# Stick-breaking attention regrouped by pairs of heads and halves of the queries in a one-core decoder layer

## The reference, cut to what matters

```python
def _stick_breaking(q, k, v):
    scale = 1.0 / math.sqrt(Dh)
    ...
        z = jnp.einsum('bqhd,bkhd->bhqk', qb, k).astype(jnp.float32) * scale
        causal = (s_pos[None, :] < t[:, None])[None, None]
        log_beta = jax.nn.log_sigmoid(z)
        log_keep = jnp.where(causal, jax.nn.log_sigmoid(-z), 0.0)
        after = lax.cumsum(log_keep, axis=3, reverse=True) - log_keep
        a = jnp.where(causal, jnp.exp(log_beta + after), 0.0)
        return jnp.einsum('bhqk,bkhd->bqhd', a.astype(v.dtype), v)
```

## Time and profile before

| | us |
|---|---|
| median of 3 runs (2522.57 to 2524.77) | 2524.6 |
| the profiled execution | 2522.39 |
| its span, first to last instruction | 2520.6 |
| PE, DVE, ACT, POOL busy in the span | 2450.4, 1169.5, 573.5, 194.7 |
| mean granted clock of TensorE | 0.985 |
| first stick-breaking scores to the end of the memory attention's turn 0 | 823.5 to 1154.4 |

### The profile page before, as it was taken

How to read it: one execution, slowest core, us unless ns; L and a number is a source line. 1 busy time by engine, 2 the same in 40 slices (tenths; PEclk the granted TensorE clock), 3 DMA queues, 4 the chain that set the end, 5 groups by cost and what they waited for, 6 DMA issues and landing times.

```text
span 2520.6 us, 25978 instructions
## 1 busy us (share of the span) xinstructions
PE 2450.4 (97%) x10608; PEld 1917.2 (76%) x10608; DVE 1169.5 (46%) x1193; ACT 573.5 (23%) x716; POOL 194.7 (8%) x153
## 2 busy tenths in 40 slices
PE   6999999999999999889999999999999999999998
PEld 5888888888887555446666888878788888888887
DVE  7344444444446556556643533353444444444444
ACT  5211111111104444442413311131311111111111
POOL 2000000000002445330000000001000000000000
PEclk8999999999999999999999999999999999999999
DMA  5211111111113000001102111122111111111112
GB/s 161 73 50 48 44 50 50 50 49 36 48 50 117 17 17 17 9 17 34 34 26 26 55 53 52 50 69 92 49 42 51 50 50 44 48 50 50 50 50 67
DMA packets 48802, 125.80 MB, mean 50 GB/s; under 512 B 4253, under 2 KB 22461, under 8 KB 48480
## 3 DMA queue, kind: packets, MB, share of 16 engines
q1 hardware_dynamic: 45660, 112.88, 14.8%
q10 hardware_dynamic: 2596, 10.89, 1.2%
q0 software_dynamic: 480, 1.10, 0.2%
HBM read 116.42 MB, written 9.87 MB: 50 GB/s over the span
## 4 chain that ended last, share of the span: by engine, by line
PE 91%; DVE 5%; ACT 2%; issue 1%; SPq 1%; DMA 0%; DVEq 0%; ACTq 0%
PE ps L1215 90%; DVE h_lo L808 1%; SPq L453 1%; DVE w_lo L801 0%; PE ps L1516 0%; ACT pr_x L583 0%; ACT pr_x L585 0%; DVE pr_x L915 0%; DVE xT L856 0%; PE ps L1463 0%; DVE d_qk L923 0%; DVE d_qk L918 0%; DVE h_lo L1146 0%; DVE xT L973 0%; DMA raw<-in_weights 0%
## 5 line engine op out<-in xcount | busy, mean ns | idle before, releaser
L1215 PE MATMUL ps<-h_hi,w_hi 128*128 128x512 f32 x2240 | 891.5, 398 | 11.5 <-DVE h_lo L808 3.8
L1215 PE MATMUL ps<-h_lo,w_hi 128*128 128x512 f32 x2240 | 876.2, 391 | 0.0
L1215 PE MATMUL ps<-h_hi,w_lo 128*128 128x512 f32 x2240 | 693.4, 391 | 0.0
L1215 PEld LDWEIGHTS ps<-h_hi,w_hi 128*128 128x128 f32 x2240 | 422.8, 189 | 131.9 <-issue 40.7
L1215 PEld LDWEIGHTS ps<-h_hi,w_lo 128*128 128x128 f32 x2240 | 422.4, 189 | 89.5
L1215 PEld LDWEIGHTS ps<-h_lo,w_hi 128*128 128x128 f32 x2240 | 423.2, 189 | 86.1 <-issue 2.2
L523 ACT ACTIVATE w_hi<-raw 128x1024 fp32r<-128x1024 f32 x196 | 204.2, 1051 | 809.0 <-PE ps L1215 798.6
L801 DVE TENSOR_TENSOR w_lo<-raw,w_hi 128x1024 fp32r<-128x1024 f32 x196 | 252.8, 1298 | 157.4 <-ACT w_hi L523 147.6
L856 DVE TENSOR_TENSOR xT<-xT,ps 128x1024 f32<-128x1024 f32 x176 | 214.6, 1219 | 182.8 <-PE ps L1215 182.8
L1215 PE MATMUL ps<-a_hi,w_hi 128*128 128x512 f32 x704 | 276.3, 393 | 5.6 <-DVE w_lo L801 4.9
L1215 PE MATMUL ps<-a_lo,w_hi 128*128 128x512 f32 x704 | 275.2, 391 | 0.0
(11 more groups left out here) (186 smaller groups left out, 1799.0 us busy)
## 6 DMA issues: line engine op xcount, KB each, us to landing
raw<-in_weights SPq DMA_DIRECT2D x196, 512.0 KB, 3.6
x_nat<-in_x SPq DMA_DIRECT2D x8, 512.0 KB, 7.5
x_keep<-xT ACTq DMA_DIRECT2D x1, 4096.0 KB, 12.5
x_back<-x_keep ACTq DMA_DIRECT2D x1, 4096.0 KB, 12.3
out<-y_nat SPq DMA_DIRECT2D x8, 512.0 KB, 3.3
toe_keep<-toe_row ACTq DMA_DIRECT2D x2, 704.0 KB, 6.2
m_nat<-in_mem SPq DMA_DIRECT2D x1, 1024.0 KB, 5.0
d_fB<-d_f_keep POOLq DMA_DIRECT2D x2, 512.0 KB, 6.8
```

Of the source, the lines that this page charges most:

```text
L1215: return pe.matmul(o, a, b, start=start, stop=stop, skip_group_check=True)
```

## The change

The loop becomes 36 steps: 3 pairs of heads by 12, of which 8 are for queries 512 to 1023 (key tiles 7 to 0) and 4 for queries 0 to 511 (key tiles 3 to 0). A step treats both heads of its pair, so it is 2 x 128, 2 x 256, 2 x 384 or 2 x 512 columns wide.
- Scores are three fp32r products per head over split q and k (hi.hi, hi.lo, lo.hi), with the mask added by an fp32r product of `ident_r` and `neg_r` on 128 columns. Splitting q and k costs an ACT copy and a DVE subtraction for each (`qk_hi`, `qk_lo`, and the `copy` branch of `proj_final`).
- z is copied out of PSUM by ACT into the place of the weights (`sb_kept`); softplus is formed from this copy, and `sb_weights` is an Exp in SBUF.
- The running sums live in PSUM pair 2 (`carry`): `sb_within` adds the triangular product, DVE adds the bank to the kept z (`sb_add`), then `sb_carry` adds the complementary triangle (the constant -1 becomes -(i<j)), so the bank then holds the whole sum. POOL has no part any more; `sum_hi`, the mask multiplication and POOL's three operations are gone.
- Pair 3 is split: one bank is the output of both heads of a half of the queries (`sb_out`, 6 copies of 128x512), the other takes the dense work as half units of 512 columns (`beside`): eight units in steps 0 to 31, 12 products in each step. The two `x_q` units get their norm by halves in steps 32 to 35.
- The first half of unit U_DIL leaves the loop: it is now made in turn 0 of the memory attention, before `sb_values` of the last step. The memory attention's units swap PSUM pairs.

```diff
             def sb_explog(s):
 
-                a = (7 - s % 8) * P
+                l, z = sb_l[:, s % 2, :, sb_step(s)[3]:], sb_scores_of(s)[:, :, sb_step(s)[3]:]
                 act.wait_ge(sb_z, s + 1)
...
+                nc.scalar.activation(l, z, ACT.Abs).then_inc(sb_abs, 1)
+                after(act, sb_av, s - 2)
+                nc.scalar.activation(sb_weights_of(s)[:, :, sb_step(s)[3]:], z, ACT.Copy).then_inc(sb_kept, 1)
                 act.wait_ge(sb_abs, s + 1)
...
+            def sb_weights(s):
+                a = sb_weights_of(s)[:, :, sb_step(s)[3]:]
+                act.wait_ge(sb_added, s + 1)
+                nc.scalar.activation(a, a, ACT.Exp).then_inc(sb_a_ready, 1)
...
+            sb_explog(0)
+            for s in range(SB_STEPS):
                 if s:
                     sb_weights(s - 1)
+                if s + 1 < SB_STEPS:
+                    sb_explog(s + 1)
+                if is_qk(half_done(s - 1)):
+                    qk_hi(half_done(s - 1))
+                if s % 4 == 0 and s < BS_STEPS:
+                    split_hi(beside_unit(s // 4) + AHEAD)
...
+            sb_softplus(0)
+            for s in range(SB_STEPS):
+                if is_v(half_done(s - 1)):
+                    v_out(half_done(s - 1))
+                if s + 1 < SB_STEPS:
+                    sb_softplus(s + 1)
+                if is_qk(half_done(s - 1)):
+                    qk_lo(half_done(s - 1))
+                if s and chain_last(s - 1):
+                    sb_out(s - 1)
+                if half_done(s) is not None:
+                    beside_copy(half_done(s))
+                if s % 4 == 0 and s < BS_STEPS:
+                    split_lo(beside_unit(s // 4) + AHEAD)
+                sb_add(s)
+                if s >= BS_STEPS:
+                    xq_scale(s - BS_STEPS)
...
+                for i, (k, q) in enumerate(((2, 0), (2, 1), (3, 0))):
+                    for h in range(2):
+                        r = h * HD
+                        last = mm(ps[:, s % 2, 512 * h + a:512 * h + 512], sb_qk[r:r + HD, p % 2, k, j * P:(j + 1) * P],
+                                  sb_qk[r:r + HD, p % 2, q, 512 * c + a:512 * c + 512], i == 0, i == 2 and j < 4 * c)
...
             sb_scores(0)
+            for s in range(SB_STEPS):
+                if s + 1 < SB_STEPS:
                     sb_scores(s + 1)
+                if is_v(half_done(s - 1)):
+                    v_turn(half_done(s - 1))
+                if s >= BS_STEPS:
+                    xq_sum(s - BS_STEPS)
                 if s:
+                    sb_carry(s - 1)
                     sb_values(s - 1)
+                if beside_half(s) is not None:
+                    beside(s)
...
+                sb_within(s)
```

More of the change, by code:

```diff
@@ L133, in proj_unit, with sb_step, chain_first, chain_last @@
 def proj_unit(n):
[L134 removed]
+    return U_MEM + n if n < PR_SB else U_SB + n - PR_SB if n < PR_DIL else U_DIL + n - PR_DIL
 def proj_pair(n):
[L138 removed]
+    return 2 if n < PR_SB else n % 2 if n < PR_DIL else 2 + (n - PR_DIL) % 2
 def aux_pair(n):
[L142 to L171, removed]
+    return proj_pair(n) if n >= PR_DIL else 3 if n < PR_SB else 2
+PAIR_STEPS, SB_STEPS = 12, 36
+def sb_step(s):
+    p, i = divmod(s, PAIR_STEPS)
+    c, j = (1, 7 - i) if i < 8 else (0, 11 - i)
+    return p, c, j, max(j * P - 512 * c, 0)
+def chain_first(s):
+    return s % PAIR_STEPS in (0, 8)
+def chain_last(s):
+    return s % PAIR_STEPS in (7, 11)
+def chains_before(s):
+    return sum(chain_last(i) for i in range(s))
+BESIDE = 8
+BS_STEPS = 4 * BESIDE
+def beside_unit(b):
+    return U_SB + 3 + b
+def beside_half(s):
+    return s // 2 if 0 <= s < BS_STEPS else None
+def half_done(s):
+    return s // 2 if s % 2 and 0 <= s < BS_STEPS else None
+def is_v(half):
+    return half is not None and half < 12 and half // 2 % 3 == 2
+def is_qk(half):
+    return half is not None and half < 12 and half // 2 % 3 < 2
+def halves_before(half, kind):
+    return sum(kind(i) for i in range(half))
 def layer(nc, x, mem, weights, gains, head_gains, rel_bias, consts, onehot, out):
@@ L694, in x_exp @@
+            sb_weights(SB_STEPS - 1)
             def x_exp(n):
@@ new lines, in sb_carry @@
+            def sb_carry(s):
+                a = sb_step(s)[3]
+                if chain_last(s):
+                    return
+                pe.wait_ge(sb_added, s + 1)
+                for part in (sp_hi, sp_lo):
+                    for h in range(2):
+                        last = mm(carry(h)[:, a:], tri[:, 1, :], part[:, s % 2, h, a:], False, True)
+                last.then_inc(sb_rest, 1)
+            def sb_values(s):
+                p, c, j, a = sb_step(s)
+                if chain_first(s):
+                    after(pe, sb_o, chains_before(s))
+                if s % PAIR_STEPS == 0 and p:
+                    pe.wait_ge(bs_v, 2 * p)
@@ L1408, in sb_values @@
                 pe.wait_ge(sb_a_ready, s + 1)
-                if j == 7:
-                    after(pe, sb_o, head)
-                for c, d in bank_pieces(j * P, S):
-                    last = mm(ps[r:r + HD, 2, c:d], sb_v[:, buf, j, r:r + HD], sb_a[:, s % 2, c:d], j == 7 or (j == 3 and c < 512), j == 0)
+                for h in range(2):
+                    r = h * HD
+                    last = mm(sb_out_bank[r:r + HD, a:], sb_v[p % 2][:, j, r:r + HD], sb_weights_of(s)[:, h, a:], chain_first(s), j == 0)
@@ new lines, in v_turn, with xq_sum @@
+            def v_turn(half):
+                c = half % 2
+                pe.wait_ge(bs_copied, half + 1)
+                for b in range(4):
+                    last = pe.transpose(beside_bank[:, b * P:(b + 1) * P], pr_x[2][:, 512 * c + b * P:512 * c + (b + 1) * P], ident)
+                last.then_inc(bs_turned, 1)
+            def xq_sum(q):
+                pe.wait_ge(xq_square, q + 1)
+                pe.wait_ge(bs_copied, 2 * BESIDE)
+                after(pe, xq_newton, 3 * q - 2)
+                mm(beside_bank, head_ones, pr_x[0][:, half_of(q)[1]], True, True).then_inc(xq_sums, 1)
```

347 lines of the change are left out of this document (186 added, 161 removed).

## The result

The changed kernel takes 2532.8 us (median of 8 runs, 2531.2 to 2540.9) beside 2523.4 for the kernel before (8 runs on the same chip): ratio 1.004, 95% interval 1.0031 to 1.005, so slower by 9 us. The profiled execution has a span of 2531.6 against 2520.6. The forecast was 2533. The sum met the result, but not all of its terms did, and the experiments were chosen to find which.

A forecast was written before the change was run, and what follows sets the result against it. PE bounded the kernel before, 97% busy; in the changed loop an ACT-DVE ring would set the pace. Ring 2.7 + clock 5 + turn 0 1.3 = +9 us on the span, giving 2533 us on the median; range 2517 to 2547.

The forecast's parts named there:

- The ring: Stick-breaking loop: ACT and DVE take turns from add to add, 10.0 us a full step; loop +2.7 us at full clock.
- the ring does not close: Rival, loop: a link is shorter, PE stays the bound with 23 us less; 2480 to 2518 us, chance 0.12.
- side by side: Rival: two heads' products overlap; PE-bound steps gain -5.5, turn 0 0.9 more; 2524 to 2529 us, chance 0.20.
- The clock: Loop: PE's waits bring 3 to 4 falls to 1.2 GHz at about 1.5 us each, +5; bounds 0 and +14.
- third rival: Loop: 8 or more clock falls at 3 us, +25, or slower 64-row fp32r products; 2544 to 2570 us, chance 0.13.
- Step 35: Last loop step: PE is the later one, 6.7 us with x_scores(0) at 1.9 in it, against 2.1 of ring.
- The loop's account: Loop: ring sum 296 us plus 17 for PE-late steps gives 313 us to the last add at full clock.
- Turn 0: After the loop's last sum, up to the memory attention's second unit: 23.3 against 22.0 us, +1.3.
- the moved half unit costs almost nothing: Turn 0: the moved half unit, 5.7 us, fills what was a wait of 4.13 us.
- Prologue: Three leading units: ACT's two copies and DVE's two subtractions lie beside 33 us of PE work, 0.

The follow-up runs named there:

- e4: Changed kernel with one more ScalarE copy of 128x1024 behind sb_explog(s+1) in steps 0 to 23: 2531.8 us, 1.0035.
- e7: Changed kernel with the three score products of one head issued before those of the other: 2531.5 us, 1.0029.
- e12: Changed kernel with 3, 10 or 6 useless 512-column products ahead of the next step's scores, in steps 1 to 32 only: 2531.9 us, 1.003.

## Why the prediction was right, point by point

**The ring: right, and shown.** Engines that take turns, full steps 10.0, PE idle ahead of `sb_carry` and released by the add, POOL empty; DVE's adds waited for PE in 6 of 36 steps. A microsecond put on the ring cost 0.95 us a full step, the same beside it nothing, and the add moved ahead opened it.

**The rival "the ring does not close": refuted** by the same runs. What it named as its price (up to 45 us if PE stays the bound) was too low: the order that opens the ring gives 67 us against the changed kernel. PE's turn is shorter than I priced, the waits of `beside_copy` can be moved too, and most falls of the clock go; how the 67 us part among these is not shown.

**The rival "side by side": its mechanism and its price are real, its total is not, because it came with many falls of the clock instead of few.** The Trainium skill has the rule (TensorEngine Tiling (Array Packing), Overview: up to twice the speed where contraction or output is 64 or less), and here the trace agrees: 0.96 us for six products, 1.08 for values that took 1.93. In the sum I had taken 0.235 us for each, by the pass count; no row of the kernel before has products of two row groups as neighbours, so the rows could not have told. Steps 7, 11, 19, 23 and 31 take 7.36, 6.65, 7.37, 6.65 and 7.36 at full clock, against 8.4, 7.7, 8.4, 7.7 and 8.4 forecast: -5.2 in sum, and 0.85 in turn 0, as the rival had it. In full ring steps it only made PE wait longer.

**The clock: the term that was mis-sized.** I took 3 or 4 falls and +5 us. There were 17 in the loop. Against the same steps at full clock they cost 2.5 in step 7, 2.7 in step 11, 2.5 in step 23, 1.6 in step 31 and 3.1 in the first step: 12.4 us. The other falls lie mostly in ring steps with slack and cost next to nothing: steps 4, 16 and 18 hold one each and take 11.13, 11.13 and 10.06, against 11.14, 11.14 and 10.01 at full clock with 12 products beside. So neither my count nor the third rival's "8 or more falls at 3 us, +25" is what happened: many falls, most of them covered, and dear where PE is late. One that hit, timeline of PE in step 7 of the changed kernel, behind its wait for the add:

```profile
888.05 1.22 PE L1315 MATMUL ps<-sp_hi,tri 128*128 128x512 f32 x2 [3.05 <-DVE sb_a L1083]
889.07 1.06 PE L1315 MATMUL ps<-sp_lo,tri 128*128 128x512 f32 x2
890.06 1.98 PE L1315 MATMUL ps<-sb_a,sb_v 128*64 128x512 f32 x4
...
892.56 0.63 PE L1315 MATMUL ps<-h_lo,w_hi 128*128 128x512 f32 x1
892.99 0.63 PE L1315 MATMUL ps<-h_hi,w_lo 128*128 128x512 f32 x1
893.41 0.47 PE L1315 MATMUL ps<-h_hi,w_hi 128*128 128x512 f32 x1
```

Starts are 0.42 us apart instead of 0.235, the values take 1.98 instead of 1.08, and the add behind them has to wait, because the next step's softplus is narrow and DVE was done early. These 12.4 us are read from the steps of one profiled execution, and they are no fixed price: in the traces of e4 and e7 the same five steps cost 9.0 us over full clock, as step 7 holds no fall and step 11 a shorter one. When the falls were filled (e12), 4 to 5 us came back against the changed kernel's trace and next to nothing against those two, so no median shows the amount.

**Step 35: a wait that I had not seen.** `xq_sum` stands ahead of `sb_carry` on PE and waits for DVE's `xq_scale` of the step before. Timelines of PE and of DVE, end of the loop:

```profile
1131.74 2.04 PE L1315 MATMUL ps<-pr_x,cst 128*128 128x512 f32 x2 [5.66 <-DVE pr_x L1126]
```
```profile
1139.38 1.22 DVE L1083 TENSOR_TENSOR sb_a<-sb_a,ps 128x1024 f32<-128x1024 f32 x1 [5.93 <-PE ps L1315]
```

`sb_carry` needs only the add of step 34, which ended at 1131.0, but it starts behind `xq_sum` at 1132.80. The step takes 9.33 us, not 6.7: +2.6, of which 1.8 is this wait and `xq_sum` itself, and the rest I put down to the half clock. No run moved `xq_sum` alone, so the parts are read from the trace only. I had followed the written orders of DVE and ACT, and not PE's own.

**The loop's account.** 313 forecast to the last add at full clock, - 5.2 + 2.6 + 12.4 = 322.8; measured 319.0 (821.6 to 1140.6, the end of the add). Of the remaining -4, 1.06 is a slip of the sum: it counts 36 Exps of the weights, and the last stands behind the last add. The rest lies in the other steps, inside the 2% (5 us) that I had set as the ring's bound, and is not traced further.

**Turn 0: +4.3, not +1.3.** (The terms as printed add up to 23.1, not 23.3.) The 22.0 of before holds 10.2 us at half clock, and its transposes take 1.94; I set full-clock prices (1.0 for them) against it. Timeline of PE, changed kernel:

```profile
1150.80 1.97 PE L1606 MATMUL ps<-cst,x_p 128*128 128x128 f32 x8 [3.39 <-DVE x_p L1057]
1152.70 3.78 PE L1315 MATMUL ps<-mkT,x_q 64*128 64x256 f32 x8
1156.41 0.79 PE L1315 MATMUL ps<-h_hi,w_hi 128*128 128x512 f32 x1
...
1163.65 1.93 PE L1315 MATMUL ps<-x_pT,mv 128*64 128x512 f32 x4
```

Transposes 1.9 instead of 1.0, scores 3.7 instead of 1.9, the half unit 7.24 instead of 5.7: +4.2 on 23.3, less 0.85 for the values side by side, is 26.65, and 26.3 were measured. With 10.2 us at half clock in both stretches, the +4.3 is what the change itself costs: the add (1.4) and the half unit (5.7) are new, the values are 0.85 and the wait ahead of the transposes 0.7 shorter, and the 1.11 us that PE waited for the weights' Exp before is gone, since that Exp now runs beside the half unit. That makes +4.4. So "the moved half unit costs almost nothing" is refuted: it does not lie in the wait of 4.13 but ahead of it, and 3.39 of that wait is still there, set anew by the division of the probabilities on DVE, which stands behind `sb_out`.

**Prologue: 0** forecast. It came out at -1.9. Of this 1.6 comes from a fall of 3.4 us at 759.7, which in these two profiled executions only the kernel before had: its lag behind the other grows there from 0.3 to 1.9 us. Other runs of this study have such a fall and others not, so this term is chance and not the change.

So 2.7 + 5 + 1.3 = 9 became a loop of +8.7, a turn 0 of +4.3 and a start of -1.9. The ring was foreseen; that the total was met so closely, 11 for 9, is luck, because terms of both signs were off: priced too low were the falls in the loop (by 7.4), the wait in step 35 (2.6) and turn 0's clock (4.2), 14 in all; not priced were side by side (-6), the start (-1.9) and the rest (-4), 12 in all.

## What to carry to other kernels

Draw the order on each engine as arrows, with the waits as further arrows, and look for a closed ring through two engines: its length is the step, however idle either engine is, and moving a few instructions in the queues can be worth more than the arithmetic that a change saves (here 67 us against 35 us of PE). When a change makes the busiest engine wait in every step, price the clock in the steps where that engine is late, not by the number of falls. And set a stretch's new price against its old one at the same clock.

## What was unexpected of the hardware

- Two products on different halves of the rows run at the same time even if they aren't issued one after the other: three of one head, then three of the other, still ended in 0.97 us; one product on all 128 rows between them made it 2.1.
- Two true fp32 products of 512 columns with 64 output columns each, in different column halves, take 1.08 us instead of 1.93; 1.98 at half clock.
- 99 us of useless work on the busiest engine cost 14.5 us, because most of it went into waits, with the clock at 2.4 GHz from 826 to 1142. In fitted amounts inside the loop (e12) the profiled span was 3.5 us shorter than without, which the medians (2531.9 and 2532.8) do not confirm.
- Ahead of the loop, where the instructions are the same, the profiled executions of this study reach the same instruction (at 812 us) up to 6 us apart. A gain of that size can't be read from one profiled span.
